# Rotary halves swapped by two matmuls instead of four ScalarE copies, and short contractions cut to their 2 and 16 rows

## The reference

```python
h = rms_norm(h_res, norm_mix_g)
dq, dk, dv, fq, fk, fv, f_logit, g_a, g_b = split_cols(h @ w_in, W_IN_SPLITS)
dq = partial_rope(rms_norm(dq.reshape(b, length, 8, 2, 64), diff_q_norm_g), cos, sin)
dk = partial_rope(rms_norm(dk.reshape(b, length, 8, 2, 64), diff_k_norm_g), cos, sin)
# partial_rope: of 64 dimensions the first 16 turn
#   x1, x2 = xr[..., :8], xr[..., 8:16];  rot = [x1*c - x2*s, x2*c + x1*s]
o_diff = (softmax(q1 k1) - lam * softmax(q2 k2)) @ v          # differential attention
s = fq fk * scale + cum_logf[q] - cum_logf[k]                  # forgetting attention
o_fox = softmax(s) @ v
```

## Time and profile before

| | |
|---|---|
| runs | 2065.29, 2063.63, 2067.13 us; median 2065.29 |
| the profiled execution's own time | 2065.29 us |
| its span, first to last instruction | 2063.5 us (1.8 us lie around it) |
| busy share of the span | PE 96%, DVE 81%, ACT 55%, POOL 34% |
| instructions | 32,519 |
| head stage | about 33 us to 577 us of the span, 66.70 us a head |

### The profile page before, as it was taken

The page is one execution under the profiler, slowest core; times in us unless marked ns, Lnnn a source line. Parts: engine busy times, 40 slices in busy tenths (PEclk is TensorE's granted clock), DMA queues, the critical chain, the costliest instruction groups (busy, mean ns, idle before and its releaser), DMA issues.

```text
span 2063.5 us, 32519 instructions
## 1 busy us (share of the span) xinstructions
PE 1981.1 (96%) x11640; PEld 1746.6 (85%) x11640; DVE 1665.3 (81%) x2351; ACT 1142.7 (55%) x1638; POOL 691.3 (34%) x352
## 2 busy tenths in 40 slices
PE   6999999999999989999999999999999999999996
PEld 4999889998988878999988989999777777777775
DVE  6765676666678556999999999977788888888886
ACT  5655565656677345655555555655455555555453
POOL 2000000000000000688888888888222221222220
PEclk9999999999999999999999999999999999999998
DMA  5555545555445545899999999999799999999996
GB/s 179 186 182 193 193 166 178 174 195 191 154 154 180 183 152 181 313 321 319 322 317 321 316 326 322 329 326 336 276 388 370 381 380 373 381 377 373 378 370 211
DMA packets 137713, 565.81 MB, mean 274 GB/s; under 512 B 44256, under 2 KB 52320, under 8 KB 88256
## 3 DMA queue, kind: packets, MB, share of 16 engines
q1 hardware_dynamic: 87440, 415.36, 55.5%
q0 software_dynamic: 49920, 147.33, 21.0%
q10 hardware_dynamic: 304, 2.62, 0.4%
HBM read 547.18 MB, written 16.88 MB: 273 GB/s over the span
## 4 chain that ended last, share of the span: by engine, by line
PE 77%; DVE 15%; issue 5%; ACT 2%; DMA 1%; DVEq 0%; SPq 0%; ACTq 0%
PE psum L751 27%; PE psum L532 16%; PE psum L730 8%; PE psum L536 8%; PE psum L733 7%; DVE wlo L430 3%; DVE xr L430 3%; PE psum L522 2%; PE psum L518 2%; PE psum L517 2%; DVE arena L1404 2%; ACT arena L860 1%; DVE arena L1457 1%; ACT whi L411 1%; DVE arena L1390 0%
## 5 line engine op out<-in xcount | busy, mean ns | idle before, releaser
L418 DVE TENSOR_TENSOR wlo<-raw,whi 128x1024 fp32r<-128x1024 f32 x242 | 293.8, 1223 | 168.7 <-PE psum L536 113.0
L730 PE MATMUL psum<-xr,whi 128*128 128x384 f32 x2048 | 381.8, 338 | 0.0
L532 PE MATMUL psum<-xr,whi 128*128 128x512 f32 x1408 | 365.4, 401 | 10.3 <-DVE xr L1333 5.8
L751 PE MATMUL psum<-whi,xr 128*128 128x512 f32 x1536 | 371.9, 391 | 3.2 <-ACT xr L1025 3.1
L730 PEld LDWEIGHTS psum<-xr,whi 128*128 128x128 f32 x2048 | 352.2, 189 | 0.2
L751 PEld LDWEIGHTS psum<-whi,xr 128*128 128x128 f32 x1536 | 289.8, 189 | 64.3 <-ACT xr L1025 3.3
L424 ACT ACTIVATE whi<-raw 128x2048 fp32r<-128x2048 f32 x169 | 322.6, 1909 | 9.8 <-DMA raw<-v_rows 6.9
L532 PEld LDWEIGHTS psum<-xr,whi 128*128 128x128 f32 x1408 | 255.0, 190 | 60.7 <-issue 7.7
L1073 POOL DMA_INDIRECT arena<-v_rows,small x64 | 143.6, 2244 | 402.0 <-DVE arena L1417 401.4
L411 ACT ACTIVATE whi<-raw 128x1024 fp32r<-128x1024 f32 x244 | 248.8, 1053 | 35.9 <-PE psum L536 18.4
L1073 POOL DMA_INDIRECT arena<-u_rows,small x64 | 125.6, 1962 | 359.1 <-DMA small<-arena 331.6
(11 more groups left out here) (244 smaller groups left out, 3107.3 us busy)
## 6 DMA issues: line engine op xcount, KB each, us to landing
raw<-stream SPq DMA_DIRECT2D x244, 512.0 KB, 3.3
raw<-v_rows SPq DMA_DIRECT2D x85, 1024.0 KB, 7.8
raw<-u_cols SPq DMA_DIRECT2D x84, 1024.0 KB, 6.4
arena<-v_rows SPq DMA_DIRECT2D x43, 1024.0 KB
arena<-u_cols SPq DMA_DIRECT2D x42, 1024.0 KB
gates<-arena POOLq DMA_DIRECT2D x8, 1536.0 KB, 9.5
small<-gates SPq DMA_DIRECT2D x62, 192.0 KB, 8.2
arena<-x_t SPq DMA_DIRECT2D x4, 544.0 KB, 6.4
```

The source lines that it names most:

```text
L418: nc.vector.tensor_tensor(wlo[:, k % 2 * HALF:(k % 2 + 1) * HALF], raw[:, s * HALF:(s + 1) * HALF], f(whi[:, s * HALF:(s + 1) * HALF]), AL ...
L532: mm(bank(b), whi[:, s * HALF + c * P:s * HALF + (c + 1) * P], both[c], start=start and c == 0, stop=False)
L730: mm(bank(at, 0, 2 * TD), hi_w[:, c * P:(c + 1) * P], z_all[:, :, c, 0:TD // TS, :], start=c == 0, stop=False)
L751: last = mm(at[:, (b * 4 + j * 2 + n) * 512:(b * 4 + j * 2 + n + 1) * 512], weights, src, start=begin, stop=end, skip_group_check=True)
```

## The change

Three things, all in the head stage:

1. The swap of the halves goes to PE. A constant 128 by 128 permutation matrix `swap` is added to the constants. At p = 4, after block 4 and ahead of the mean squares, PE waits for `head_normed` and issues two float32 matmuls of `swap` with dq (256 columns, into bank 5) and dk (272 columns, into bank 6). DVE's sine product reads the result from PSUM in place of `rope_a`. ACT's four copies are gone. The tables and the host's column order go back to the plain one.
2. The forget-term matmuls contract over 2 rows, the meta-key matmuls over 16, in place of 128.
3. With that no zero rows are needed: the memset of `padded` and the two waits for it are gone, and `v`, `pT`, `cum_q`, `cum_k` are placed differently in SBUF. The constants grow by 128 columns (64 KB).

```diff
-          ("mean128", P), ("ident", P), ("one", 1), ("rows01", 3),
+          ("mean128", P), ("swap", P), ("ident", P), ("one", 1), ("rows01", 3),
...
+        for j in range(8):
+            swap[b + j + 8, b + j] = 1.0
+            swap[b + j, b + j + 8] = 1.0
...
# PE
                     if p == 4:
+                        pe.wait_ge(head_normed, i * 2 + 1)
+                        mm(bank(5, 512 - T, T), C["swap"], piece("dq"), start=True, stop=True)
+                        mm(bank(6, 0, L), C["swap"], piece("dk"), start=True, stop=True).then_inc(rot_done, 1)
                         pe.wait_ge(bank_free, i * PER_HEAD + 6)
...
-                            last = mm(acc, cum_q[:, n * P:(n + 1) * P], cum_k[:, 0:keys], start=False, stop=True)
+                            last = mm(acc, cum_q[0:2, n * P:(n + 1) * P], cum_k[0:2, 0:keys], start=False, stop=True)
...
-                        mm(bank(2, j * T, T), v[j][:, 0:P], pT[j][:, 0:T], start=True, stop=False)
+                        mm(bank(2, j * T, T), v[j][0:META, 0:P], pT[j][0:META, 0:T], start=True, stop=False)
# ACT
-            act.wait_ge(padding_set, 1)
...
-                    if p == 4:
-                        act.wait_ge(head_normed, i * 2 + 1)
-                        for a, b in ((0, 32), (32, 0), (64, 96), (96, 64)):
-                            last = A(rope_a[a:a + 32, :], qk[b:b + 32, 0:T + L], ACT.Copy)
-                        last.then_inc(rot_done, 1)
# POOL
-            nc.gpsimd.memset(padded, 0.0).then_inc(padding_set, 1)
# DVE
-            dve.wait_ge(padding_set, 1)
...
-                            ch.link(V.tensor_tensor(rope_a, rope_a, C["rope_sin"], ALU.mult))
+                            ch.link(V.tensor_tensor(rope_a, psum[:, 6 * 512 - T:6 * 512 + L], C["rope_sin"], ALU.mult))
# host
-    half = np.r_[0:8, 16:40, 8:16, 40:64]
-    turned = np.r_[half, 64 + half]
-    dq, dk = (w.reshape(D, HEADS, P)[:, :, turned].reshape(D, n) for w in (dq, dk))
```

More of the change, by code:

```diff
@@ L105, in shape_constants @@
     cc, ss = np.ones((P, L), np.float32), np.zeros((P, L), np.float32)
+    swap = np.zeros((P, P), np.float32)
     for b in (0, 64):
-        cc[b:b + 8], cc[b + 32:b + 40] = cos, cos
-        ss[b:b + 8], ss[b + 32:b + 40] = -sin, sin
+        cc[b:b + 8], cc[b + 8:b + 16] = cos, cos
+        ss[b:b + 8], ss[b + 8:b + 16] = -sin, sin
+        for j in range(8):
+            swap[b + j + 8, b + j] = 1.0
+            swap[b + j, b + j + 8] = 1.0
     put("rope_cos", np.concatenate([cc[:, META:], cc], 1))
@@ L117, in shape_constants @@
     put("mean2048", 1.0 / 2048)
+    put("swap", swap)
     put("ident", np.eye(P))
@@ L214, in hybrid_layer @@
         r_low = low.sub(MID - low.a)
-        r_work = high.sub(NK * T - MID - c_w - P - 2 * HEADS * T)
+        r_work = high.sub(NK * T - MID - c_w - 2 * HEADS * T)
         r_o = high.sub(2 * HEADS * T)
-        high.take(P)
         c_sb = high.take(c_w)
@@ L242, in hybrid_layer @@
         rope_a, rope_b = w1.take(T + L), qk_sq[:, 0:T + L]
+        v = [w1.take(384) for _ in range(2)]
         cum_rows = r_low.again().take(HEADS * L)
         o_sq, o_std = small[:, T + L:2 * T + L], small[:, 2 * T + L + SC_W:3 * T + L + SC_W]
-        padded = w1.sub(768 + T + L + 2 * 640)
-        cum_q, cum_k = padded.take(T), padded.take(L)
+        cum_q, cum_k = small[:, 0:T], w1.take(L)
         vT = [w1.take(L), small[:, T:T + L]]
         prob = [w1.take(SC_W) for _ in range(2)] + [small[:, 2 * T + L:2 * T + L + SC_W]]
-        v = [padded.take(384) for _ in range(2)]
-        pT = [padded.take(640) for _ in range(2)]
-        padded = padded.again().take(768 + T + L + 2 * 640)
+        pT = [w1.take(640) for _ in range(2)]
         sm = w1.take(24)
@@ L386, in hybrid_layer @@
             sem("head_scores_ready"), sem("head_scores_taken"), sem("head_best_ready"), sem("head_best_exp"))
-        padding_set = sem("padding_set")
         zero_set, zeroed, picked = sem("zeros_set"), sem("gates_zeroed"), [sem(f"picks_ready{b}") for b in range(2)]
@@ L1538, in lay_out @@
     put("b_gate", inputs["b_gate"][0].reshape(2 * KC, P).T)
-    put("g_dq", np.tile(inputs["diff_q_norm_g"][0][half], 2)[:, None])
-    put("g_dk", np.tile(inputs["diff_k_norm_g"][0][half], 2)[:, None])
+    put("g_dq", np.tile(inputs["diff_q_norm_g"][0], 2)[:, None])
+    put("g_dk", np.tile(inputs["diff_k_norm_g"][0], 2)[:, None])
     put("g_fq", inputs["fox_q_norm_g"][0][:, None])
```

## The result

| | before | after |
|---|---|---|
| median of 6 runs, us | 2065.88 | 2080.32 |
| lowest to highest, us | 2063.63 to 2067.13 | 2078.89 to 2082.57 |
| span of the profiled execution, us | 2063.5 | 2078.1 |

The ratio, which takes in all 29 runs of the changed kernel, is 1.0075, 95% interval 1.0065 to 1.0085: the changed kernel is slower by 0.75%, some 15 us (the two medians of the table lie 14.4 us apart). The forecast was slower by 0.46%, 2074.9 us, with a range to 2079.0 us. The direction was right, the size was not; 2080.3 us lies 1 us under what the rival with the dearer switch gave (2081.3 us).

A forecast was written before the change was run, and what follows sets the result against it. PE was taken to bound the head stage: +0.89 for the swap, -0.41 for the lost wait, +0.72 for switches make +1.20 us a head, times 8 heads +9.6 us on 2065.3, so 2074.9 us; range 2068 to 2079 us.

The forecast's parts named there:

- the rival with the dearer switch: Head stage: each change of row count costs PE 0.19 us, net 2.00 us a head, 2081.3 us; chance 0.08.
- What bounds the stage: Head stage: PE, idle 0.34 us of a 66.70 us turn; whatever enters its stream is paid in full, eight times.
- The two swap matmuls: End of block 4 on PE: two float32 matmuls of 256 and 272 columns add 0.89 us a head.
- Their new wait: End of block 4: PE's stop for `head_normed` costs nothing, as DVE is done about 2 us earlier.
- The wait that goes: Differential scores: without ACT's copies PE no longer waits for DVE's last rope addition; 0.41 us a head comes back.
- PSUM as the source: DVE's sine product reading 528 columns from PSUM takes 0.7 to 0.9 us, inside 4 us of room: costs nothing.
- Fewer rows, the small matmuls themselves: Forget-term and meta-key matmuls: contracting over 2 and 16 rows makes them no shorter, zero gain.
- I take 0.09 us a switch, both ways: Forget-term and meta-key matmuls: eight changes of row count a head at 0.09 us each, +0.72 us a head.
- Memset, waits, constants: Before the head stage: dropping the memset and its two waits, and loading 64 KB more constants, changes nothing.
- no switching cost: Rival: contractions of 2 and 16 rows cost no switch, net +0.48 us a head, 2069.1 us; chance 0.18.
- cheap short matmuls: Rival: few-row matmuls run beside their 128-row neighbours and their steps vanish, net -1.09 us a head, 2056.6 us; chance 0.08.

The follow-up runs named there:

- grouped: The changed kernel with both full forgetting-score products first and both 2-row ones behind them; 68.24 us a head, 2076.82 us, ratio 1.0054 to the kernel before.
- rows_only: The kernel before with only the forget-term and meta-key contractions cut to 2 and 16 rows, ACT's copies kept; 68.13 us a head, 2075.96 us, ratio 1.0053.
- swap_only: The changed kernel with all contractions over 128 rows again, padded and its memset and waits kept; 67.17 us a head, 2069.15 us, ratio 1.0018 to the kernel before.

## Why the prediction was wrong, step by step

- *What bounds the stage*: right. Every term, up or down, came through in the turn to within 0.04 us a head.
- *The two swap matmuls, +0.89 us*: measured 0.89. *Their new wait, nothing*: no idle time. *The wait that goes, -0.41 us*: measured 0.41. The sum of these was forecast at +0.48 and measured at +0.47 a head.
- *PSUM as the source*: 0.70 us, the lower of the two bounds (0.7 and 0.9 us), with about 4 us of room as forecast.
- *Fewer rows, the small matmuls themselves*: zero gain, right; grouped shows no price and no gain for 2-row matmuls among their own, and 2, 16 and 64 rows give the same turn.
- *"I take 0.09 us a switch, both ways", +0.72 us a head*: this is the step that failed. That a switch costs, how many there are and where they stand were right; the term was half of what it should have been. Measured: 1.43 us for eight (rows_only), 0.18 us each on average, against 0.72 and 0.09. The two rows I compared end at the first matmul on the new rows, so they hold only what is paid ahead of it; that the two directions agreed to 0.01 us, which spoke against the dearer switch, showed only that both left out the same part. The other 0.10 us comes one step later, between the first and the second record. With the term at its measured size the sum is 0.48 + 1.43 = 1.91 us a head, 15.3 us, 2080.6 us. That this second 0.10 us exists is measured; that it is the load of weights in the open is read from the load rows and from the 16-column case, and no run tested it.
- The second part could have been read beforehand, one step behind the last of the earlier trace rows. In narrow stretches of the trace of before:

```profile
796.61 0.73 PE L532 MATMUL psum<-xr,whi 128*128 128x512 f32 x2
796.95 0.62 PE L532 MATMUL psum<-xr,whi 128*128 128x512 f32 x2
```

  Each row holds two matmuls: the first the one behind the 64-row scores and its follower, the second begins with that follower: 0.34 us from one to the next, where 512 columns otherwise take 1.86 us for eight, 0.23 each. I had set the upper bound at 0.19 us, but then gave that end 0.08 and cut the range at 0.155 us.
- *Memset, waits, constants*: nothing that can be seen. They act ahead of the first head, so the turns say nothing of them; the first head's start moves by up to 2 us between kernels, but not with the memset (50.4 us in swap_only, which has it; 51.6 us in grouped, which has not), and an effect smaller than that scatter stays open.
- *The rivals*: no switching cost (2069.1 us) and cheap short matmuls (2056.6 us) fell with rows_only and grouped. The dearer switch (2081.3 us), which had a chance of 0.08, is nearly what happened: 1.90 us a head net where it had 2.00.

The Trainium skill (TensorEngine Tiling (Array Packing), Key Properties) has the mechanism of the first part, that a change of the tiling mode drains TensorE; the 0.09 us ahead of the first matmul on new rows agrees with it. The two levels at 64 and 96 rows agree with its list of modes in the same page (Tiling Modes: 64-row and 32-row tiles below the full 128); the size is this case's own, 0.18 us on average.

## What to carry to other kernels

In a saturated matmul stream like this one, contracting over fewer rows saved nothing, and each step between full-height matmuls and ones of 2, 16 or 64 rows cost 0.18 to 0.19 us. So leave small operands padded with zeros to the full height where they stand among full ones, or put the short ones together (which saved its two switches here, in an order that would still have to be made to sum rightly). To price a disturbance in a pipelined stream, compare the whole stretch from before it until the steps are ordinary again, and not only the one step at which it shows. And before work is moved onto the engine that bounds the stage to shorten a wait, try to start the work earlier where it is: here that gave the same 0.41 us a head for nothing.

## What the runs showed of the hardware that was not expected

- The price of a change of rows is in two parts, 0.09 us and 0.10 us; the second was missing where the next stationary operand had 16 columns.
- It has two levels: 2, 16 and 64 rows cost the same to 0.02 us a head, 96 rows cost the same as 128.
- A DVE product of 528 columns takes 0.70 us with one source in PSUM across two banks, and 0.71 us with both in SBUF.
